# One conditioning sum order and six table loads: a two-block transformer kernel on one Trainium2 core

## The reference, cut to what matters

```
mod = silu(c) @ w_ada + b_ada                    # 1024 -> 6144 = 12 groups of 512 columns
h   = rms_norm(x, g) * (1 + sc) + sh             # 6 such norms: two per layer, called norm 0 to norm 5
x   = x + g1 * mixer(h)                          # short convolution / neighbourhood attention / sparse attention + RWKV
x   = x + g2 * feed_forward(h)                   # SwiGLU of width 2816 in layers 0 and 1, 32 experts in layer 2
```

## Time and profile before

| | before |
|---|---|
| median of 3 runs | 2047.9 us (2043.93 to 2051.4) |
| profiled execution, its own time | 2051.34 us |
| span of its profile | 2049.6 us, mean granted clock 0.981 |
| PE busy | 1959.3 us |
| DVE / ACT / POOL busy | 840.7 / 280.8 / 290.2 us |
| mean DMA rate | 204 GB/s, in the last stage about 428 GB/s |

### The profile page before, as it was taken

How to read it: one execution, slowest core, us unless ns; L and a number is a source line. 1 busy time by engine, 2 the same in 40 slices (tenths; PEclk the granted TensorE clock), 3 DMA queues, 4 the chain that set the end, 5 groups by cost and what they waited for, 6 DMA issues and landing times.

```text
span 2049.6 us, 25515 instructions
## 1 busy us (share of the span) xinstructions
PE 1959.3 (96%) x10686; PEld 1323.7 (65%) x10686; DVE 840.7 (41%) x1402; ACT 280.8 (14%) x596; POOL 290.2 (14%) x258
## 2 busy tenths in 40 slices
PE   6999999999999999988999999989997999999998
PEld 3444468888778874457788888768786544455444
DVE  2566338888874345192434213674324100000001
ACT  2000020000000121162000011241202100000000
POOL 0001115555532220000111010400000000000000
PEclk9999999999999999999999999989997999999999
DMA  9545105554341350004876451320026999999997
GB/s 400 191 164 186 61 21 165 163 164 163 143 173 57 146 244 0 0 1 174 347 256 227 166 229 44 128 104 24 24 82 246 395 426 429 428 428 428 429 428 314
DMA packets 48781, 420.22 MB, mean 205 GB/s; under 512 B 5440, under 2 KB 5456, under 8 KB 22960
## 3 DMA queue, kind: packets, MB, share of 16 engines
q1 hardware_dynamic: 29376, 344.73, 41.4%
q0 software_dynamic: 18880, 71.18, 10.4%
q10 hardware_dynamic: 432, 2.96, 0.4%
HBM read 417.81 MB, written 1.05 MB: 204 GB/s over the span
## 4 chain that ended last, share of the span: by engine, by line
PE 75%; DVE 11%; DMA 9%; issue 3%; ACT 2%; DVEq 0%; SPq 0%; ACTq 0%; POOLq 0%
PE PS L1258 8%; PE PS L1388 8%; PE PS L992 7%; DMA ring<-w_moe 6%; PE PS L1035 6%; DVE SC L1782 6%; PE PS L1099 5%; PE PS L1443 4%; PE PS L1409 4%; PE PS L1025 4%; PE PS L1246 4%; PE PS L1084 4%; PE PS L1422 3%; PE PS L1119 3%; PE PS L1216 2%
## 5 line engine op out<-in xcount | busy, mean ns | idle before, releaser
L1258 PE MATMUL PS<-ring,A 128*64 128x512 f32 x1024 | 223.6, 593 | 3.8 <-DMA ring<-w_moe 2.9
L1258 PEld LDWEIGHTS PS<-ring,A 128*64 128x64 f32 x1024 | 73.9, 137 | 150.3 <-issue 141.4
L1782 DVE SCALAR_TENSOR_TENSOR SC<-A,CS,SC 128x512 f32<-128x512 f32 x208 | 164.8, 845 | 5.6 <-DMA A<-ada 3.7
L1388 PE MATMUL PS<-A,ring 128*128 128x512 f32 x368 | 159.7, 594 | 0.0
L1025 PE MATMUL PS<-A,ring 128*128 128x256 f32 x704 | 158.0, 386 | 1.2 <-ACT A L586 1.2
L992 PE MATMUL PS<-ring 128*128 128x256 f32 x672 | 152.4, 383 | 0.0
L1025 PEld LDWEIGHTS PS<-A,ring 128*128 128x128 f32 x704 | 135.1, 193 | 24.3 <-issue 5.8
L992 PEld LDWEIGHTS PS<-ring 128*128 128x128 f32 x672 | 127.8, 191 | 26.1 <-issue 8.9
L1388 PEld LDWEIGHTS PS<-A,ring 128*128 128x128 f32 x368 | 69.4, 190 | 89.8 <-issue 89.8
L445 POOL DMA_DIRECT2D ring<-ada x64 | 34.9, 546 | 575.8 <-DVE SC L1782 358.1
L1246 PE MATMUL PS<-ring,A 128*64 128x512 f32 x512 | 113.4, 595 | 0.7 <-ACT A L685 0.7
(11 more groups left out here) (360 smaller groups left out, 2523.7 us busy)
## 6 DMA issues: line engine op xcount, KB each, us to landing
ring<-w_moe SPq DMA_DIRECT2D x96, 2048.0 KB, 18.5
ring<-w_fin SPq DMA_DIRECT2D x44, 1024.0 KB, 7.0
ring<-ada POOLq DMA_DIRECT2D x64, 512.0 KB, 4.1
A<-ada POOLq DMA_DIRECT2D x64, 512.0 KB, 4.6
ring<-w_fout SPq DMA_DIRECT2D x16, 1408.0 KB, 7.2
ring<-w_conv SPq DMA_DIRECT2D x8, 1536.0 KB, 14.5
ring<-w_qkv SPq DMA_DIRECT2D x6, 2048.0 KB, 15.2
ring<-w_win SPq DMA_DIRECT2D x6, 2048.0 KB, 10.5
```

The lines of the kernel that those rows point to most:

```text
L1258: mm = pe.matmul(PS[CAP * e:CAP * (e + 1), g, :], XG[:, k * P + e * CAP:k * P + (e + 1) * CAP], slot("moe", k // 2, w, w + 512), start=(k ...
L1388: mm = pe.matmul(PS[:, 3 * (j % 2) + c, :], slot("conv", j, k * 384 + c * 128, k * 384 + c * 128 + 128), h_of(k, 512), start=(k == 0), sto ...
L1782: ins = dve.scalar_tensor_tensor(out=ACC[:, i, :], in0=w, scalar=scale, in1=ACC[:, i, :], op0=ALU.mult, op1=ALU.add)
```

## The change

ACT's program gets a helper that runs the wanted function on one column of a small new tile, TAB, for nothing but its table. It is called with Sqrt at the beginning of norm 2 to 5 and before the group norm's square, and with Exp before the first value copy. On PE, the sum of group 9 moves out of slot 21 of the first feed-forward into the first step of its output product, and the sums of the second feed-forward move from the odd slots 1, 3, 5, 7, 9 to the even slots 2, 4, 6, 8, 10.

```diff
+        TAB = sb("TAB", 2)
...
+            def table(func):
+                act.activation(TAB[:, 0:1], eps, func)
+
             def norm(n):
                 c0, layer, s2, cond = NORMS[n]
                 T = s2 * SEQ
+                if n > 1:
+                    table(ACT.Sqrt)
                 for k in range(KD):
...
                 relu_pair(3 + j)
+            table(ACT.Exp)
             value_copy(0, 0)
...
             gate_raw(4, 5)
+            table(ACT.Sqrt)
             act.wait_ge(sem("centred"), 1)
...
                     fold(b + 2, 0, f[:, 0], FH4[:, 0])
-                    if s >= 3 and s % 2:
+                    if s >= 3 and s % 2 and s < 21:
                         ada_sum(1, (s - 3) // 2)
...
                         mm.then_inc(sem("product"), 1)
-                        if s in (1, 3, 5, 7, 9):
-                            ada_sum(2, 5 * it + s // 2)
+                        if s in (2, 4, 6, 8, 10):
+                            ada_sum(2, 5 * it + s // 2 - 1)
...
                     fold(b + 1, 1, w0[:, 11:22], HID4[:, 11:22, 1, :])
+                    if i == 0:
+                        ada_sum(1, 9)
```

## The result

The changed kernel takes 2031.1 us, the median of five runs (2028.0 to 2033.9); the kernel before took 2047.7 us beside it. The ratio is 0.9922, 95% interval 0.9906 to 0.9939, that is 12.5 to 19.2 us less. A second measurement of the same kernel, further down, gives 2033.2 us and 0.9929 (0.9916 to 0.9943). The forecast was 2036.0 us with 2029 to 2043: faster, as said, and inside the range, but by 16.6 us instead of 11.9 (15.0 in the second measurement). The profiled execution took 2033.85 us, with a span of 2032.2.

A forecast was written before the change was run, and what follows sets the result against it. PE, busy for 96% of the span, was taken as the bound, so only its waits could be won: 3.9 + 5.3 + 0.6 + 2.1 = 11.9 us off the median 2047.9 gives 2036.0 us, range 2029 to 2043.

The forecast's parts named there:

- Part A: First feed-forward: moving group 9's sum out of slot 21 removes a PE stop; 3.9 us gained, bounds 0 and 5.7.
- Rival 1: First feed-forward: slot 21 is bound by DVE in full, so moving its sum gains 0; 2039.9 us, chance 12%.
- The upper bound of 5.7: First feed-forward's output product: 3.9 us plus 1.8 us if the slow clock behind PE's 1.96 us wait goes too.
- Part B: Second feed-forward: sums one slot later remove the late sum's stop, 5.3 us, and hide the last sum, 0.6 us.
- The late sum's 5.3: Second feed-forward, slot 3: moving the late sum gains 5.3 us, 3.7 of wait and 1.6 of slower clock behind it.
- the last wait's 0.6: End of the second feed-forward: group 9's sum hides in PE's wait for DVE's last hidden block, 0.6 us gained.
- Rival 4: Second feed-forward: the late sum's wait returns a group later, as the next parts land late too; 2041.3 us, chance 10%.
- Rival 5: Second feed-forward: conditioning-weight loads fall into a chain and eight more sums stop PE; 36 us slower, 2084, chance 2%.
- Part C: Norms 3 to 5 and group norm: early table loads let roots start sooner; 2.1 us gained, bounds 0 and 5.3.
- Rival 2: Table loads don't move where it counts, through compiler placement or a chain bound by PE's sums; 2038.1 us, chance 9%.
- rival 3: The clock dips less after the shorter stops, at 581 and in a norm: 2 x 1.7 us more, 2032.6, chance 13%.

The follow-up runs named there:

- A alone: Only the sum of group 9 moved, from slot 21 of the first feed-forward to its output product, against the kernel before: 2044.4 us, ratio 0.9981.
- B alone: Only the sums of the second feed-forward moved one slot later, against the kernel before: 2039.4 us, ratio 0.9959.

## Why the prediction was right, and where it was short

**Part A was right**: 3.9 us forecast, 3.8 in the trace, 3.6 in the medians of A alone. The chain was the forecast one: L487 went from 569.14 to 564.88, which is 3.9 us when the 0.38 is taken off by which DVE's group itself starts earlier (556.11 to 555.73); the last hidden block ends 0.56 us behind POOL's L488 (568.62 and 568.06) where 0.55 was assumed; stops of 1.87 and 1.42 us in A alone where 1.7 and 1.3 were written; the sum hidden, the gain set by DVE's copies. Rival 1 (A gives 0) is out. What was written for it, that DVE has no idle time between group 9 and the copies, was misread: before the change DVE was idle for 4.10 us there, ahead of L1924 at 569.09, waiting for PE's last fold. That is why the chain could move. The upper bound of 5.7 was built on a slow stretch that, as B alone shows, comes or stays away by itself. My expectation for A alone put weight on it again, and it was wrong: 2044.4 is the value of the rival without it.

**Part B was mis-sized**, and this is the term of the sum that failed. I wrote 5.3 + 0.6 = 5.9 us; the stage gave 7.36. The late sum's 5.3 is right (5.05 with one sum moved, group 2's new wait of 0.45 included) and the last wait's 0.6 too (0.54). What is missing is in the sentence "The other nine are small and stand elsewhere or stay". It is true of the nine that the list of waits shows: they belong to the first feed-forward and still cost 3.0 us. But the ten sums of the second each waited 0.14 us that no list shows, 1.4 us in all. I had even taken 14.69 us as the interval of "undisturbed" slots, where an undisturbed one is 14.55. With it the terms are 5.3 + 0.54 + 1.4 = 7.2 us. Rival 4, the wait that comes back a group later, is out: in the changed kernel no sum of this stage waits, and even with one sum moved and group 2 in its old slot, that one waited 0.45 us. DVE's timeline in the changed kernel shows parts of group 1 and of group 2 landing late, as the earlier trace rows did, only that PE no longer notices:

```profile
990.46 1.54 DVE L1793 SCALAR_TENSOR_TENSOR SC<-A,CS,SC 128x512 f32<-128x512 f32 x2 [2.25 <-DMA A<-ada]
...
1001.74 1.54 DVE L1793 SCALAR_TENSOR_TENSOR SC<-A,CS,SC 128x512 f32<-128x512 f32 x2 [2.20 <-DMA A<-ada]
```

Group 1 ends at 992.0, 2.4 us ahead of its sum. Rival 5, the chain that makes it slower, never began.

**Part C was right** to the hundredth: 0.87, 0.87, 0.20, nothing in norm 2 and at Exp, some 0.26 in the group norm where at most 0.18 was written. Rival 2 is out. The sentence that in norm 2 squares stand ahead of the root "with no load in between" was no support for it, since in the kernel before a load stood exactly there, at 709.88 behind the last square. That none is needed the changed kernel shows: load at 674.27, squares from 697.72, root at 705.27. The cover was better than forecast. I costed norm 2's new load at 1.5 us inside ACT's idle 1.98; it runs 23 us earlier, and the idle time is 1.88 still. The Trainium skill (ScalarE: Activation LUTs, What ACT_TABLE_LOAD costs) counts a drain of 1.38 us beside the load. In every norm here the root came directly behind its load, and the gains are those of the load alone, so no drain shows. Its rule that Copy and Relu are in every set (Table sets: the hidden batching unit) agrees: as many loads as before, 18.

**Everything reached the end**: the turns of the last stage wait for slots as before, 0.73 us.

**The sum** with B as measured is 3.8 + 7.4 + 2.2 = 13.4 us. The two measurements give 16.6 (12.5 to 19.2) and 15.0 (11.7 to 17.2), and both intervals hold 13.4; the three parts alone add up to 3.6 + 8.6 + 2.1 = 14.3 in medians. The profiled spans differ by more, 17.4, and what lies beyond 13.4 is in stages that are as short in a profile without the change (above). That was luck of the profile, and no confirmation of rival 3, whose slow stretches were to go because of the shorter stops. In the measurements the clock has a part too. An estimate of it is (1 - granted clock) x span, from the clock listed for each run: on average 38 us in 40 runs of the kernel before and 32 us in the ten of the changed kernel. So some 6 of about 15 us go with the clock. Some of that is in the rows, since both long stops had a slow stretch behind them; the rest isn't tied to any stop, and whether the last one to three us are the change's stays open.

## What to carry to other kernels

A sum that gathers another engine's results costs nothing when it stands in a wait that is there anyway; find out which engine that wait is for, because moving work out of one stop tends to show that engine's next delay (here DVE's copies), and a wait for less, or a reordering on that engine, then gives some more (here 1.7 and 3.0 us, counted up to norm 2). Compare the intervals between equal steps with what their work takes, and not only with one another: a wait of 0.14 us in every step stands in no list. Price the slow clock behind a stop from several profiles: behind stops of 3.7 to 4.0 us it stood each time here (1.5 us and more) and was rightly counted at the late sum; behind stops of 1.9 us it stood only now and then, and there one profile says little.

## What the runs showed of the hardware that wasn't expected

- **A table load doesn't wait for the activation that it serves.** In norm 2 the load ran at 674.27 us, when ACT's work before it was done; its activation waited for PE until 697.61. A load in front of a waiting instruction can thus be hidden already, as in norm 2, and an early one only pays where ACT comes to it late.
- **The same stop, two outcomes.** A wait of 1.96 us ahead of the same 44 instructions was followed by 11.42 us (clock 0.50) before, and by 9.73 us in B alone. After a wait of 1.87 us the next 22 instructions took 5.01 us, and after one of 1.88 they took 6.70. Of the eight profiled stops of 1.85 to 1.97 us at these two places three had a slow stretch behind them; of the seven of 3.7 to 4.0 us (slot 21 in four profiles, the late sum in three) all had one.
- **The parts land late wherever the sum stands.** DVE waited 2.24 us for the last part of group 1 before and 2.25 after, at a DMA share of about 1. What moving the sum changed is only that PE no longer waits for DVE there.
